# A 1024-to-4096-to-1024 MLP: fifteen instead of thirteen pairs by seven products, and fifteen tile remainders on GpSimd

## The chip, the cores and the metric

The kernel runs on one core of a Trainium2 chip, as one launch. The metric is the time of one execution on the device in microseconds; the number compared is the median over several executions. A core has a matrix engine (TensorE; PE in the profile, with its weight loads as PEld), three engines for elementwise work (VectorE, DVE; ScalarE, ACT; GpSimd, POOL) and SyncE (SP), which here issues the loads of weights. The engines run their own instruction lists and meet only at semaphores.

## The reference, cut to what matters

Two transformer blocks run one after the other on 256 tokens of width 1024, all in float32. The change is in the MLP that ends the first block:

```python
x = x + mix @ w_out[layer]
h = rmsnorm(x, norm_mlp[layer])
x = x + jnp.square(jax.nn.relu(h @ w_up[layer])) @ w_down[layer]   # 1024 -> 4096 -> 1024
```

The second block (norm `norm_mix_2`, projections `w_in_2`, ...) starts from this `x`.

## The kernel before

**Precision.** TensorE multiplies in a reduced format (fp32r). Each operand is therefore kept as two parts: a rounded one, `h`, and its remainder `l` = operand - `h`. One product takes three matmuls: h·h, h·l and l·h. For a tile of weights, ScalarE makes `h` (`round_tile`, line 1111) and VectorE makes `l` (`rest_of_tile`, line 1661).

**Tiles and rings.** `weight` asks for a tile of 512 KB. SyncE loads it into one of RAW = 4 slots of `raws`, in the order in which TensorE asks for tiles (line 2585); before it loads a slot again it waits until the tile that was there has its remainder (semaphore `lo`). `h` and `l` go to one of PARTS = 5 buffers of `parts`; ScalarE rounds tile i only when TensorE has released tile i-5. ScalarE and VectorE take all tiles in this one order. Between two pieces of other work, `until(v)` lets them first take the tiles whose buffer TensorE gives back before its event v; a tile whose buffer comes free exactly at v comes after that piece.

**The MLP.** The 4096 hidden columns are 16 pairs q of 256. For each pair TensorE computes `up(q)` from two tiles of `w_up` (48 matmuls of 256 columns). ScalarE takes relu and square of it (lines 1392, 1394) and rounds it (1399), VectorE makes the remainder (1695). Then pair q meets rows 256q to 256q+255 of `w_down`, in two tiles: `down(q, 0)` for output columns 0 to 511, `down(q, 1)` for 512 to 1023. TensorE runs up(q), down(q-2, 0), down(q-2, 1) in turn. The loop ends with up(15) and down(13, 0); then come down(14, 0), down(15, 0), down(13, 1), the transposes of the first half of the new x (`turn_x`, line 490), down(14, 1), down(15, 1).

**Seven products.** In the form with 12 matmuls of 512 columns (lines 806 to 808), down(q, 0) is a product of 2 x 2 blocks with eight block products. For the pairs in `by_sums` (1 to 13 here) `down_by_sums` takes seven, from sums of blocks: 21 matmuls of 256 columns (line 764). The sums of weight blocks are made by VectorE (`sums_of`, lines 1714 to 1718) and count as one more tile in the ring of five, rounded by ScalarE and given its remainder by VectorE. The sums of activation blocks are made by GpSimd (lines 2450 to 2454), rounded by ScalarE (1379) and given their remainder by VectorE. Two products are held in banks of their own; after the last pair by sums ScalarE copies one block (`first_copied`, 1384), VectorE adds the rest up (`join`) and adds all of the first half to x (line 1701). Only then may TensorE transpose it.

Of the kernel before, what the change touches and what calls it, by code (L numbers as in the profile page):

```python
# [48 lines left out]
    "qk_hi", "qk", "w_sums", "u_sums", "us_hi", "usT", "first_product", "joined",  # L49
# [10 lines left out]
class Tile:  # L60


    def __init__(self, i, srcs, k, n, raw, h, l):
        self.i, self.srcs, self.k, self.n = i, srcs, k, n
        self.raw, self.h, self.l = raw, h, l
        self.slot = self.load = self.before = None
        self.sums = self.nth_sums = None
        self.release = None
# [34 lines left out]
def build(nc, a, out):  # L103
    with ExitStack() as ctx:  # L104
# [123 lines left out]
        by_sums = [range(1, 14), range(1, 10)]  # L228
# [3 lines left out]
        us = [[chunks(v[:, :, :].rearrange("p c n -> p (c n)"), 4) for v in pair(17664 + 1024 * i, 2)] for i in range(4)]  # L232
        joint = f32(21760, 256)
# [74 lines left out]
        tiles, loaded, made = [], [], []  # L308
# [6 lines left out]
        def tensor(e):  # L315
# [39 lines left out]
            def weight(src, k, n, paired=False):  # L355

                i, slot = len(tiles), len(loaded) % RAW
                raw = raws[:, slot, 0:k * n].rearrange("p (k n) -> p k n", k=k)
                h, l = (parts[:, i % PARTS, j, 0:k * n].rearrange("p (k n) -> p k n", k=k) for j in range(2))
                if paired:  # L360
                    srcs = [(raw[64 * g:64 * g + 64], src[64 * k * g:64 * k * (g + 1), :].rearrange("(k p) n -> p k n", p=64))
                            for g in range(2)]
                else:
                    srcs = [(raw, src.rearrange("(k p) n -> p k n", p=P))]
                t = Tile(i, srcs, k, n, raw, h, l)
                t.slot, t.before = slot, loaded[-RAW] if len(loaded) >= RAW else None
                t.load = 16 * len(srcs) + (t.before.load if t.before else 0)
                tiles.append(t)
                loaded.append(t)
                return t  # L370
# [383 lines left out]
            def mlp(u, n, up, w_down):  # L754
# [12 lines left out]
                def down_by_sums(q):  # L767
# [15 lines left out]
                    product(c11, u12, w21)  # L783
# [10 lines left out]
                    sums.release = done(product(c21, u22, t4))  # L794

                def down(q, h):
# [3 lines left out]
                    w_ = weight(w_down[256 * q:256 * q + 256, 512 * h:512 * h + 512], 2, 512)  # L800
                    need(s["lo"], w_.i + 1)
                    for t in range(2):
                        ps, tok = psum[:, own[2 * h + t], :], slice(t * P, t * P + P)
                        for k in range(2):
                            wh, wl, (uh, ul) = w_.h[:, k, :], w_.l[:, k, :], ups[q % 4]
                            e.matmul(ps, uh[:, k, tok], wh, start=q == 0 and k == 0, stop=False)  # L806
# [7 lines left out]

                for q in range(2, n):
# [275 lines left out]
        def scalar(e):  # L1091
# [294 lines left out]

            def up(q):
                until(where["up", q].at)
                sums_rounded(0, q - 1)
# [9 lines left out]
                e.activation(ups[q % 4][0], r, ACT.Copy).then_inc(s["up_hi"], 1)  # L1399

            for q in range(16):
                up(q)
            first_copied(0)
# [240 lines left out]
        def vector(e):  # L1644
# [118 lines left out]

            def residual(name, u, factor=None, factor_in=None, n=0):
# [16 lines left out]
                if late:  # L1781
                    rest_of_tile()
                gains(u, 0, late)
                if late:
                    rest_of_tile()
                rests(u, 0)
                if late:
                    rest_of_tile()
# [4 lines left out]
                if late:  # L1793
                    rest_of_tile()
# [264 lines left out]
            for q in range(16):  # L2059
                r, name = tmps[q % 4], ("up", q)  # L2060
                until(where[name].at)
                sums_rest(0, q - 1)
                full(name)
                e.wait_ge(s["up"], q + 1)
                rest(r, ups[q % 4], "up_hi", q + 1, "upT")
            e.wait_ge(s["gain2"], 1)
# [346 lines left out]
        def gpsimd(e):  # L2413
# [41 lines left out]

            def all_up_sums(u):

                for q in by_sums[u]:
                    if u:
# [39 lines left out]
            all_up_sums(0)  # L2499
            e.wait_ge(s["xT"], 4 * MIX2 + 4)  # L2500
# [72 lines left out]
        def sync(e):  # L2573
# [100 lines left out]
```

## Time and profile before

| | us |
|---|---|
| median of 3 executions | 954.05 (953.63 to 955.58) |
| the profiled execution, its own time | 953.48 |
| its span in the trace | 951.3 |
| TensorE busy | 943.1 (99% of the span) |
| VectorE busy | 701.3 (74%) |
| ScalarE busy | 558.4 (59%) |
| GpSimd busy | 128.5 (14%) |

The span is what the trace covers; the 2.2 us by which the execution is longer lie around it. The MLP of the first block takes the stretch from 219 to 389 us. A time of the trace is counted from the start of the span.

### The profile page before, as it was taken

The page shows a single profiled execution, that of the slowest core. Times are in us where ns is not written, and L with a number is a line of the kernel's source. Part 1 is how long each engine was busy: PE and PEld are TensorE (multiplying, and loading weights), DVE is VectorE, ACT ScalarE, POOL GpSimd, SP SyncE. Part 2 cuts the span into 40 slices and gives each one's busy share as a digit, 9 for nine tenths or more (in the row PEclk, how much of TensorE's full clock was granted, in tenths as well). Part 3 has the DMA queues.
Part 4 walks back from the last instruction along what each step waited for, and adds up shares of the span by engine and source line. Part 5 has one row for each costly group of instructions (what it writes and reads, how often), then busy time and mean ns, then how long its engine had stood idle before and what let it go on. Part 6 is the DMA issues. An engine that isn't in the chain of part 4 may idle for free. (4 is left out here: it accounts for less than half of the span.)

```text
span 951.3 us, 16977 instructions
## 1 busy us (share of the span) xinstructions
PE 943.1 (99%) x6888; PEld 868.2 (91%) x6888; DVE 701.3 (74%) x934; ACT 558.4 (59%) x852; POOL 128.5 (14%) x178
## 2 busy tenths in 40 slices
PE   9999999999999999999999999999999999999997
PEld 7877999989999999989987999998998899999996
DVE  6767875777777887888866787776666467777777
ACT  6577554556666666656865674545455445555544
POOL 3000001004223320414000001100000012121210
PEclk9999999999999999999999999999999999999999
DMA  9974447555666666656565365555645346565661
GB/s 309 305 242 130 118 128 179 159 177 185 191 190 194 194 195 202 181 160 199 146 188 162 106 202 175 176 182 172 196 162 171 118 156 201 176 201 177 199 200 66
DMA packets 133549, 170.43 MB, mean 179 GB/s; under 512 B 5824, under 2 KB 97296, under 8 KB 133472
## 3 DMA queue, kind: packets, MB, share of 16 engines
q1 hardware_dynamic: 131408, 165.07, 55.9%
q10 hardware_dynamic: 1424, 2.84, 0.9%
q0 software_dynamic: 640, 1.44, 0.7%
q8 instruction: 54, 0.88, 0.4%
q14 instruction: 23, 0.19, 0.1%
HBM read 168.28 MB, written 1.05 MB: 178 GB/s over the span
## 5 line engine op out<-in xcount | busy, mean ns | idle before, releaser
L1661 DVE TENSOR_TENSOR parts<-raws,parts 128x1024 fp32r<-128x1024 f32 (+3 forms) x307 | 364.5, 1202 | 131.3 <-ACT parts L1111 130.4
L1111 ACT ACTIVATE parts<-raws 128x1024 fp32r<-128x1024 f32 (+3 forms) x307 | 309.3, 1029 | 129.2 <-PE ps L405 54.2
L403 PE MATMUL ps<-room_r,parts 128*128 128x256 f32 x1248 | 351.6, 282 | 0.0
L404 PE MATMUL ps<-room_r,parts 128*128 128x256 f32 x1248 | 348.6, 279 | 0.0
L405 PE MATMUL ps<-room_r,parts 128*128 128x256 f32 x1248 | 348.3, 279 | 0.0
L403 PEld LDWEIGHTS ps<-room_r,parts 128*128 128x128 f32 x1248 | 234.6, 188 | 2.2 <-issue 0.8
L404 PEld LDWEIGHTS ps<-room_r,parts 128*128 128x128 f32 x1248 | 234.7, 188 | 1.1
L405 PEld LDWEIGHTS ps<-room_r,parts 128*128 128x128 f32 x1248 | 234.7, 188 | 0.0
L434 PE MATMUL ps<-parts,room_r 128*128 128x512 f32 (+1 forms) x336 | 133.9, 399 | 0.8 <-DVE parts L1661 0.8
L435 PE MATMUL ps<-parts,room_r 128*128 128x512 f32 (+1 forms) x336 | 131.1, 390 | 0.0
L436 PE MATMUL ps<-parts,room_r 128*128 128x512 f32 (+1 forms) x336 | 131.1, 390 | 0.0
L434 PEld LDWEIGHTS ps<-parts,room_r 128*128 128x128 f32 x336 | 63.1, 188 | 16.2 <-DVE parts L1661 2.1
L436 PEld LDWEIGHTS ps<-parts,room_r 128*128 128x128 f32 x336 | 63.1, 188 | 14.4
L435 PEld LDWEIGHTS ps<-parts,room_r 128*128 128x128 f32 x336 | 63.2, 188 | 13.4 <-issue 0.5
L1695 DVE TENSOR_TENSOR room_r<-room,room_r 128x512 fp32r<-128x512 f32 (+1 forms) x71 | 49.4, 696 | 32.0 <-ACT room_r L1399 10.2
L764 PE MATMUL ps<-parts,room_r 128*128 128x256 f32 x462 | 58.1, 281 | 0.0
L764 PEld LDWEIGHTS ps<-parts,room_r 128*128 128x128 f32 x462 | 56.0, 188 | 0.0
L1111 ACT ACTIVATE parts<-room 128x1024 fp32r<-128x1024 f32 x22 | 23.4, 1062 | 55.2 <-DVE room L1718 30.1
L806 PE MATMUL ps<-parts,room_r 128*128 128x512 f32 x116 | 46.1, 397 | 0.0
L807 PE MATMUL ps<-parts,room_r 128*128 128x512 f32 x116 | 45.9, 395 | 0.0
L808 PE MATMUL ps<-parts,room_r 128*128 128x512 f32 x116 | 45.7, 394 | 0.0
L2450 POOL TENSOR_TENSOR room<-room 128x256 f32<-128x256 f32 x22 | 16.2, 738 | 207.9 <-DVE room L1695 116.3
(241 smaller groups left out, 1115.1 us busy)
## 6 DMA issues: line engine op xcount, KB each, us to landing
raws<-in_w_in SPq DMA_DIRECT2D x99, 512.0 KB, 4.4
raws<-in_w_ffn_in SPq DMA_DIRECT2D x44, 512.0 KB, 4.4
raws<-in_w_up SPq DMA_DIRECT2D x32, 512.0 KB, 3.9
raws<-in_w_down SPq DMA_DIRECT2D x32, 512.0 KB, 3.8
raws<-in_w_ffn_out SPq DMA_DIRECT2D x22, 512.0 KB, 4.4
raws<-in_w_xkv SPq DMA_DIRECT2D x16, 512.0 KB, 4.4
raws<-in_w_out SPq DMA_DIRECT2D x8, 512.0 KB, 4.3
raws<-in_w_up_ssd SPq DMA_DIRECT2D x8, 512.0 KB, 5.5
```

Of the source, the lines that this page charges most:

```text
L403: e.matmul(ps, wh, hT[0][:, k, :], start=k == 0, stop=False)
L404: e.matmul(ps, wh, hT[1][:, k, :], start=False, stop=False)
L405: last = e.matmul(ps, wl, hT[0][:, k, :], start=False, stop=k == K - 1)
L434: e.matmul(ps, hT[0][:, k, tok], wh, start=k == 0, stop=False)
L435: e.matmul(ps, hT[0][:, k, tok], wl, start=False, stop=False)
L436: last = e.matmul(ps, hT[1][:, k, tok], wh, start=False, stop=k == K - 1)
L764: last = e.matmul(ps, left[lh], right[rh], start=begins, stop=ends_)
L806: e.matmul(ps, uh[:, k, tok], wh, start=q == 0 and k == 0, stop=False)
L807: e.matmul(ps, uh[:, k, tok], wl, start=False, stop=False)
L1111: e.activation(t.h, t.raw, ACT.Copy).then_inc(s["hi"], 1)
L1661: e.tensor_tensor(t.l, t.raw, t.h.bitcast(F32), ALU.subtract).then_inc(s["lo"], 1)
L1695: return e.tensor_tensor(o, i0, i1, op)
```

## The change

1. For the first block's MLP `by_sums` covers pairs 0 to 14 instead of 1 to 13. Pair 15 stays in the usual form, with its first matmul into one bank split in two halves.
2. The second-half tiles of pairs 1 to 15 no longer go through the ring of five. `weight_apart` gives them a raw slot like any tile, but `h` and `l` lie in three places of their own. ScalarE rounds them in `apart_rounded`, one in each `up(q)` from q = 2 on, ahead of its work on up(q), and the last one after up(15). GpSimd makes their remainders in `rest_apart` (semaphore `own_lo`), each ahead of the activation sums of a pair, and the last two after all sums. SyncE waits for `own_lo` where the slot held such a tile.
3. TensorE asks for the tile of pair q-2 ahead of up(q) (from q = 3 on), for that of pair 14 ahead of down(14, 0) and for that of pair 15 ahead of down(15, 0). Loads are issued in that order.
4. VectorE's four remainders between the pieces of the residual (`rest_of_tile`) are now made only if the tile's buffer comes free in time (`due_rest`).

```diff
-        by_sums = [range(1, 14), range(1, 10)]
+        by_sums = [range(15), range(1, 10)]
+        at_apart = (10240, 12288, 24576)
...
+            def weight_apart(src):
+                slot, at = len(loaded) % RAW, at_apart[len(apart) % 3]
...
+                t.slot, t.before = slot, loaded[-RAW]
+                t.load = 16 + t.before.load
+                apart.append(t)
+                loaded.append(t)
...
-                    w_ = weight(w_down[256 * q:256 * q + 256, 512 * h:512 * h + 512], 2, 512)
-                    need(s["lo"], w_.i + 1)
+                    if h and q in asked:
+                        w_ = asked[q]
+                        need(s["own_lo"], w_.nth_apart)
+                    else:
+                        w_ = weight(w_down[256 * q:256 * q + 256, 512 * h:512 * h + 512], 2, 512)
+                        need(s["lo"], w_.i + 1)
...
                 for q in range(2, n):
+                    if q > 2:
+                        ask(q - 2)
                     up(q)
                     down(q - 2, 0)
                     if q < n - 1:
                         down(q - 2, 1)
+                ask(n - 2)
                 down(n - 2, 0)
+                ask(n - 1)
                 down(n - 1, 0)
...
+            def apart_rounded(n):
+                t = apart[n]
+                e.wait_ge(landed[t.slot], t.load)
+                if n >= 3:
+                    e.wait_ge(s["pe"], apart[n - 3].release)
+                e.activation(t.h, t.raw, ACT.Copy).then_inc(s["own_hi"], 1)
+
             def up(q):
                 until(where["up", q].at)
-                sums_rounded(0, q - 1)
+                if q > 2:
+                    sums_rounded(0, q - 1)
+                if q > 1:
+                    apart_rounded(q - 2)
                 full(("up", q))
...
             for q in range(16):
                 up(q)
+            apart_rounded(14)
             first_copied(0)
...
+            def due_rest(u):
+                if gives_back(lo) < where["tail", u].at:
+                    rest_of_tile()
...
+            def rest_apart(n):
+                t = apart[n]
+                e.wait_ge(s["own_hi"], n + 1)
+                e.tensor_tensor(t.l, t.raw, t.h.bitcast(F32), ALU.subtract).then_inc(s["own_lo"], 1)
...
                 for q in by_sums[u]:
+                    if u == 0 and q > 1:
+                        rest_apart(q - 2)
...
             all_up_sums(0)
+            for n in (13, 14):
+                rest_apart(n)
...
-                    e.wait_ge(s["lo"], t.before.i + 1)
+                    if t.before.nth_apart:
+                        e.wait_ge(s["own_lo"], t.before.nth_apart)
+                    else:
+                        e.wait_ge(s["lo"], t.before.i + 1)
```

Below, a tile D14 is the first-half tile of pair 14, S14 the sums made from it, H14 the second-half tile of pair 14 as the kernel before has it, A14 the same tile in the kernel after, and C0, C1, C2 are the first tiles of `w_in_2` for the next block.

ScalarE (ACT) at the end of the MLP. Before: D13 (its sums S13 in the row after), D14, D15, the three steps on up(15), H13, H14, the copy of the block for `join`:

```order
L1111 ACTIVATE parts<-raws 128x768 [waits s_pe,s_landed3]
L1111 ACTIVATE parts<-room 128x1024 [waits s_pe,s_w_sums]
L1111 ACTIVATE parts<-raws 128x1024 [waits s_pe,s_landed0]
L1111 ACTIVATE parts<-raws 128x1024 [waits s_pe,s_landed1]
L1392 ACTIVATE room<-ps 128x512 [waits s_pe]
L1394 ACTIVATE room<-room 128x512 [waits s_taken5]
L1399 ACTIVATE room_r<-room 128x512 [waits s_up,s_pe]
L1111 ACTIVATE parts<-raws 128x1024 [waits s_pe,s_landed2]
L1111 ACTIVATE parts<-raws 128x1024 [waits s_pe,s_landed3]
L1384 ACTIVATE room<-ps 128x256 [waits s_pe]
```

After: D14, S14, the sums of pair 14, the tile apart of pair 14 (A14), the three steps on up(15), A15, D15, C0, C1, C2, the copy:

```order
L1143 ACTIVATE parts<-raws 128x768 [waits s_pe,s_landed2]
L1143 ACTIVATE parts<-room 128x1024 [waits s_pe,s_w_sums]
L1411 ACTIVATE room_r<-room 128x512 [waits s_u_sums]
L1425 ACTIVATE room_r<-raws 128x1024 [waits s_pe,s_landed1]
L1435 ACTIVATE room<-ps 128x512 [waits s_pe]
L1437 ACTIVATE room<-room 128x512 [waits s_taken4]
L1442 ACTIVATE room_r<-room 128x512 [waits s_up,s_pe]
L1425 ACTIVATE room_r<-raws 128x1024 [waits s_pe,s_landed3]
L1143 ACTIVATE parts<-raws 128x1024 [waits s_pe,s_landed0]
L1143 ACTIVATE parts<-raws 128x1024 [waits s_pe,s_landed1]
L1143 ACTIVATE parts<-raws 128x1024 [waits s_pe,s_landed2]
L1143 ACTIVATE parts<-raws 128x1024 [waits s_pe,s_landed3]
```

D15 stood ahead of the steps on up(15) and now stands behind them and behind A15; three tiles of the next block now stand ahead of the copy that `join` waits for.

VectorE (DVE) at the same place, from the remainder of up(15) on. Before, D15 is already done there, and H13 and H14 come ahead of `join`:

```order
L1695 TENSOR_TENSOR room_r<-room,room_r 128x512 [waits s_up_hi,s_up,s_pe]
L1661 TENSOR_TENSOR parts<-raws,parts 128x1024 [waits s_hi,s_mlp_rstd,s_gain2]
L1661 TENSOR_TENSOR parts<-raws,parts 128x1024 [waits s_hi]
L1695 TENSOR_TENSOR room<-ps,room 128x256 [waits s_first_product]
L1695 TENSOR_TENSOR room<-room,ps 128x256 [waits s_dve_step]
```

After, D15 and then C0, C1 and C2 come ahead of `join`:

```order
L1741 TENSOR_TENSOR room_r<-room,room_r 128x512 [waits s_up_hi,s_up,s_pe]
L1707 TENSOR_TENSOR parts<-raws,parts 128x1024 [waits s_hi,s_mlp_rstd,s_gain2]
L1707 TENSOR_TENSOR parts<-raws,parts 128x1024 [waits s_hi] x3
L1741 TENSOR_TENSOR room<-ps,room 128x256 [waits s_first_product]
L1741 TENSOR_TENSOR room<-room,ps 128x256 [waits s_dve_step]
```

Two remainders behind up(15) have become four, and three of them are of tiles of the next block.

SyncE (SP) in the kernel after, from the load of A14 on: A14, D14 and A15, D15, then C0, C1, C2, C3:

```order
L2651 DMA raws<-in_w_down 128x2x512 [waits s_own_lo]
L2651 DMA raws<-in_w_down 128x2x512 [waits s_lo] x2
L2651 DMA raws<-in_w_down 128x2x512 [waits s_w_sums,s_lo]
L2651 DMA raws<-in_w_in_2 128x4x256 [waits s_own_lo]
L2651 DMA raws<-in_w_in_2 128x4x256 [waits s_w_sums,s_lo]
L2651 DMA raws<-in_w_in_2 128x4x256 [waits s_own_lo]
L2651 DMA raws<-in_w_in_2 128x4x256 [waits s_lo]
```

In the kernel before, the same place reads:

```order
L2585 DMA raws<-in_w_down 128x2x512 [waits s_w_sums,s_lo]
L2585 DMA raws<-in_w_down 128x2x512 [waits s_lo] x3
L2585 DMA raws<-in_w_down 128x2x512 [waits s_w_sums,s_lo]
L2585 DMA raws<-in_w_down 128x2x512 [waits s_lo]
L2585 DMA raws<-in_w_in_2 128x4x256 [waits s_lo] x4
```

The load of A14 waits for GpSimd's remainder of A13, that of C0 for A14's and that of C2 for A15's; each holds up the loads behind it.

## Rows read from the trace of the kernel before

**Rows 1.** The page: busy time of TensorE, and its granted clock in 40 slices.
```profile
PE 943.1 (99%) x6888; PEld 868.2 (91%) x6888; DVE 701.3 (74%) x934; ACT 558.4 (59%) x852; POOL 128.5 (14%) x178
PEclk9999999999999999999999999999999999999999
```
**Rows 2.** Waits of TensorE in the whole span: total us, times, longest.
```profile
PE ps L386 <- DVE junk L1842: 1.0, 1, 1.0
PE ps L434 <- DVE parts L1661: 0.8, 1, 0.8
```
**Rows 3.** Timeline of TensorE, both forms of down: start, us, what, count.
```profile
229.39 0.39 PE L806 MATMUL ps<-parts,room_r 128*128 128x512 f32 x1
...
240.58 2.65 PE L764 MATMUL ps<-parts,room_r 128*128 128x256 f32 x21
243.06 0.40 PE L806 MATMUL ps<-parts,room_r 128*128 128x512 f32 x1
...
245.86 0.28 PE L403 MATMUL ps<-room_r,parts 128*128 128x256 f32 x1
```
**Rows 4.** Busy time of the engines over one pair in the steady stretch.
```profile
251.45:262.33 10.88, 10.88 (x83) 10.34 (x82) 8.70 (x11) 7.02 (x10) 3.04 (x3) 1.00 0.64 193
```
**Rows 5.** Timeline of ScalarE at the start: the rounding of up(1).
```profile
226.53 0.63 ACT L1399 ACTIVATE room_r<-room 128x512 fp32r<-128x512 f32 x1
```
**Rows 6.** Timeline of ScalarE, last pairs: start, us, line, idle before.
```profile
360.17 0.61 ACT L1379 ACTIVATE room_r<-room 128x512 fp32r<-128x512 f32 x1
...
370.08 1.06 ACT L1111 ACTIVATE parts<-raws 128x1024 fp32r<-128x1024 f32 x1 [1.66 <-PE ps L405]
371.42 0.60 ACT L1392 ACTIVATE room<-ps 128x512 f32<-128x512 f32 x1 [0.27 <-PE ps L405]
...
372.78 0.63 ACT L1399 ACTIVATE room_r<-room 128x512 fp32r<-128x512 f32 x1
...
375.21 0.37 ACT L1384 ACTIVATE room<-ps 128x256 f32<-128x256 f32 x1
```
**Rows 7.** Timeline of TensorE at the end of the MLP.
```profile
371.22 2.65 PE L764 MATMUL ps<-parts,room_r 128*128 128x256 f32 x21
...
382.11 1.04 PE L490 MATMUL ps<-ident,x 128*128 128x128 f32 x8
```
**Rows 8.** Timeline of VectorE: sums of weight blocks, then join and adds.
```profile
364.78 0.69 DVE L1714 TENSOR_TENSOR room<-raws 128x512 f32<-128x512 f32 x1
...
366.30 0.95 DVE L1661 TENSOR_TENSOR parts<-raws,parts 128x768 fp32r<-128x768 f32 x1
...
376.77 0.42 DVE L1695 TENSOR_TENSOR room<-ps,room 128x256 f32<-128x256 f32 x1
...
379.67 1.41 DVE L1701 SCALAR_TENSOR_TENSOR x<-ps,ssq,x 128x512 f32<-128x512 f32 x2
```
**Rows 9.** Groups by form, 237 to 369 us: VectorE's remainder of a tile.
```profile
L1661 DVE TENSOR_TENSOR parts<-raws,parts 128x1024 fp32r<-128x1024 f32 x37 | 45.4, 1228 | 15.3 <-ACT parts L1111 15.3
```
**Rows 10.** Groups of GpSimd by form: its two-input operations, large and smallest.
```profile
L2450 POOL TENSOR_TENSOR room<-room 128x256 f32<-128x256 f32 x22 | 16.2, 738 | 207.9 <-DVE room L1695 116.3 <-ACT room L1394 91.6
...
L2515 POOL TENSOR_TENSOR ssq<-ssq 128x1 f32<-128x1 f32 x2 | 0.4, 186 | 0.0
```
**Rows 11.** SyncE's loads, 355 to 400 us: from issue to landing.
```profile
DMA to landing us min/median/max: 3.5/4.1/5.2
```
**Rows 12.** Timeline of ScalarE: two tiles rounded as they land.
```profile
401.82 1.06 ACT L1111 ACTIVATE parts<-raws 128x1024 fp32r<-128x1024 f32 x1 [2.75 <-DMA raws<-in_w_in]
403.20 1.06 ACT L1111 ACTIVATE parts<-raws 128x1024 fp32r<-128x1024 f32 x1 [0.32 <-DMA raws<-in_w_in]
```
**Rows 13.** Line 1714 on VectorE, all 22: ns, shortest, median, longest.
```profile
L1714 DVE TENSOR_TENSOR room<-raws x22: 677/944/951, 232.9 to 925.3; 128x512 f32<-128x512 f32 x22
```
**Rows 14.** End of the span: busy times, granted clock, DMA share, GB/s.
```profile
944.00:946.00 2.00, 1.05 (x9) 0.84 (x8) 1.26 (x3) 1.03 (x3) 0.78 (x3) 1.00 0.00 0
...
948.00:951.30 3.30, 0.00 (x0) 0.00 (x0) 0.16 (x1) 0.20 (x1) 0.00 (x0) 0.50 0.41 159
```

More of the change, by code:

```diff
@@ L66, in __init__ @@
         self.slot = self.load = self.before = None
-        self.sums = self.nth_sums = None
+        self.sums = self.nth_sums = self.nth_apart = None
         self.release = None
@@ L307, in build @@
         where = {}
-        tiles, loaded, made = [], [], []
+        tiles, loaded, made, apart = [], [], [], []
         def gives_back(i):
@@ L369, in weight @@
                 loaded.append(t)
+                return t
+            def weight_apart(src):
+                slot, at = len(loaded) % RAW, at_apart[len(apart) % 3]
+                raw = chunks(raws[:, slot, :], 2)
+                h, l = (chunks(room_r[:, i:i + 1024], 2) for i in (at, at + 1024))
+                t = Tile(None, [(raw, src.rearrange("(k p) n -> p k n", p=P))], 2, 512, raw, h, l)
+                t.slot, t.before = slot, loaded[-RAW]
+                t.load = 16 + t.before.load
+                apart.append(t)
+                loaded.append(t)
+                t.nth_apart = len(apart)
                 return t
@@ L782, in down_by_sums @@
                     product(p1, u11, w11, first)
-                    product(c11, u12, w21)
+                    product(c11, u12, w21, first and q == 0)
                     need(s["usT"], nth_sums[u][q] + 1)
@@ L793, in down_by_sums @@
                         ends(last, ("product", u, 1), sums_in[1])
-                    sums.release = done(product(c21, u22, t4))
+                    sums.release = done(product(c21, u22, t4, first and q == 0))
                 def down(q, h):
@@ L805, in down @@
                             wh, wl, (uh, ul) = w_.h[:, k, :], w_.l[:, k, :], ups[q % 4]
-                            e.matmul(ps, uh[:, k, tok], wh, start=q == 0 and k == 0, stop=False)
+                            if h == 0 and t and k == 0 and q == by_sums[u][-1] + 1 and 0 in by_sums[u]:
+                                for c in (slice(0, 256), slice(256, 512)):
+                                    e.matmul(ps[:, c], uh[:, k, tok], wh[:, c], start=False, stop=False)
+                            else:
+                                e.matmul(ps, uh[:, k, tok], wh, start=q == 0 and k == 0, stop=False)
                             e.matmul(ps, uh[:, k, tok], wl, start=False, stop=False)
@@ L813, in down, with ask @@
                         where["down", u, q] = Group(None, count, None)
+                asked = {}
+                def ask(q):
+                    if u == 0:
+                        asked[q] = weight_apart(w_down[256 * q:256 * q + 256, 512:D])
                 for q in range(2, n):
+                    if q > 2:
+                        ask(q - 2)
                     up(q)
```

18 lines of the change are left out of this document (12 added, 6 removed).

## The prediction

> **What bounds the kernel now.** First the page: TensorE is busy 99% of the span and its granted clock is full in every slice [rows 1]. Then its waits: in the whole span there are two, of 1.0 and 0.8 us [rows 2]. So nothing that another engine does faster can shorten this kernel; a gain has to come from fewer matmul columns, and any new wait of TensorE is a loss in full. Then the cost of the two forms of down: seven products take from 240.58 to 243.06, 2.48 us, the usual form from there to 245.86, 2.80 us [rows 3]. A pair in the steady stretch takes 10.88 us, in which VectorE is busy 8.70, ScalarE 7.02, GpSimd 3.04 [rows 4]. What is left to read is how far ahead of TensorE the others are at the end of the MLP, since there the order changes most. I count from T, the start of down(13, 0), which is 371.22 [rows 7]. Before, ScalarE rounds D15 at 370.08 (T-1.1), takes up(15) from 371.42 and ends with it at 373.41 (T+2.2) [rows 6]; TensorE needs D15 after one product by sums and one in the usual form, at T + 2.48 + 2.80 = T+5.3 [rows 3]. VectorE's join and adds run from 376.77 to 379.67 + 1.41 = 381.08, 4.3 us, and TensorE transposes x at 382.11 (T+10.9) [rows 7, 8]. The transposes thus have a cover of only 1.0 us.
>
> **What the change saves.** Two pairs go from 2.80 to 2.48 us: 2 x 0.32 = 0.64 us on TensorE, all of it on the path. The split matmul of pair 15 costs nothing: two of 256 columns for one of 512, and the two forms take 0.118 us for the one (2.48 / 21) and 0.233 for the other (2.80 / 12) [rows 3]. VectorE loses 15 remainders of 1.23 us [rows 9]; as TensorE does not wait for it, this is worth nothing by itself.
>
> **GpSimd's new step.** No row shows GpSimd on 128 x 1024. Its nearest row is 128 x 256 with two inputs, 0.74 us; its smallest two-input operation takes 0.19 [rows 10]. Below, it could be as fast as VectorE, 1.23 us [rows 9]; above, four times 0.74 = 2.95. I take the row with one fixed part: 0.19 + 4 x (0.74 - 0.19) = 2.4 us, which lies near the upper end because GpSimd's own row is the nearer one. The Trainium skill ("GPSIMD Engine Reference", section "Performance versus the Vector engine") gives 4497 ns for a float32 tensor_tensor of 2048, an estimate of 2.25 us for 1024; the sum below would be 0.3 us less by it. No run so far shows that size.
>
> **Steady stretch: no cost.** GpSimd has 3.04 + 2.4 = 5.4 us of work in 10.9. VectorE has 8.70 - 1.23 = 7.5 plus what GpSimd takes from it. That it takes something shows in line 1714: 677 ns at the shortest, 944 at the median, when GpSimd works beside it [rows 13]. Even if VectorE stands for the whole new step it has 7.5 + 2.4 = 9.9 of 10.9 us. The ring of five now serves four tiles a pair, so it runs further ahead. ScalarE's work on up(q) starts 1.6 us later (sums 0.6, tile apart 1.0), but up(q) is needed only two pairs on. I take 0.
>
> **Start: no cost, at most 0.5.** Pair 0 now needs its sums at 229.39 + 0.7 us. ScalarE's work on up(1) ends at 227.16 [rows 5], and the rounding (0.6) and remainder (0.7) of the sums fit behind it; GpSimd's 3.0 us for them [rows 4] run from the square of up(0), a whole step of ScalarE earlier. Tighter is the second tile of up(3), which ScalarE rounds after up(2), its sums and the first tile apart: by the lengths of such steps it is ready within 0.5 us of when TensorE wants it (229.39 + 2.48 + 2.80 + 1.40 = 236.07) [rows 3]. I take 0 and keep 0.5 for the range.
>
> **End of the MLP: here the change loses.** Three things meet, all in the order of the lists. (a) The load of A14 waits for GpSimd's remainder of A13, and D14's load stands behind it. A13 is rounded around up(14), whose matmuls end at T-10.9. ScalarE rounds up(15)'s second tile, the sums and A13 until T-9.4; GpSimd is done at T-7.0; A14 is issued then, D14 some 1.1 later, and lands after 4.1 us and behind A14 [rows 11], the landings being 1.4 us apart (401.82, 403.20) [rows 12]: T-1.5. (b) VectorE makes the sums of D14, 1.6 us (364.78 to 366.30, with a little idle) [rows 8]: T+0.1. ScalarE rounds S14 (1.06), the sums of pair 14 (0.6), A14 (1.0), and only then takes up(15), 2.0 us [rows 6]: T+4.7. A15 follows, T+5.7, then D15, T+6.7; VectorE needs 1.23 [rows 9]: D15 is ready at T+7.9, or up to T+9.3 if GpSimd's remainder of A15 holds VectorE. TensorE wants it at T + 2 x 2.48 = T+5.0. **First new wait: 3 to 4 us.** (c) join now stands behind C0, C1 and C2 on VectorE, and the block's copy behind them on ScalarE. C2's load waits for the remainder of A15: rounded T+5.7, GpSimd 2.4 and a little to start, T+8.2; issued, landed after 4.1: T+12.4; rounded and the block copied (0.37) [rows 6]: T+13.8; VectorE's remainder of C2 T+14.7; join and adds 4.3 [rows 8]: **T+19.0**. TensorE would be there at T+7.9 + 5.6 = T+13.5 to T+14.9 and waits again, **4 to 5 us**, for x. Transposes at T+19.0 instead of T+10.9 is 8.1 us late. The saving on pair 14 is swallowed by these waits; that on pair 0 stays, 0.32. Behind the transposes the work is that of before, and the tiles of the next block are further ahead. The sum is 8.1 - 0.3 = +7.8 us, on the profiled execution's 953.48: 961.3. The median of the runs is 0.57 above that execution: **961.8 us**, 0.8% slower.
>
> **Bounds of it.** Low: D14 lands in time and S14 is rounded when its buffer comes free, as D15's was at T-1.1 [rows 6], which takes 1.25 off; GpSimd at 1.23 takes 1.2 off, a landing of 3.5 [rows 11] 0.6: +4.7, 958.8. High: GpSimd at 2.95 twice, +1.1; landings of 5.2 twice, +2.2; 0.5 at the start: +11.6, 965.6.
>
> **Rivals.** (1) **The change works as it says and costs nothing**: -0.64 us, 953.4, no change that can be told. It needs D15 ready by T+5.0 and join begun by T+10.5 - 4.3 = T+6.2. Even with loads and GpSimd at no cost, ScalarE reaches D15 at T+4.4, since up(15) and A15 stand ahead of it, so it is ready at T+6.6; that speaks against it. It is right if I misread which tiles stand where. Chance 0.07. The same reading error with a lower end than that is all that is left for a real gain, 0.03. (2) **The clock falls in the waits.** At the end of the span TensorE stops at 945.05, the granted clock is still 1.00 up to 946 and is 0.50 (1.2 GHz) from 948 [rows 14]: an idle of some 3 us was followed by the lower level. The second wait here is 4 to 5 us. If the 5.6 us of matmuls behind it run at the lower level in part, it costs up to 5.6 us, say half: 961.8 + 2.8 = 964.6. Against it: if the clock falls in the first wait already, down(15, 0) and down(13, 1) fill part of the second and the price vanishes in it. Chance 0.20. (3) **VectorE becomes the bound of the steady stretch**, held by GpSimd: it decides from a GpSimd step over 10.9 - 7.5 = 3.4 us, outside my bounds; at 4 us it costs 0.6 us in 13 pairs, 8 us on top, 970. The Trainium skill ("SBUF — State Buffer", section "SBUF: two separate sides") says that the shared port pair is an exclusive lock for the whole instruction, against a VectorE operation with two SBUF inputs; by it VectorE does stand for the full step, which I have counted, and the first wait is the longer one of the two I give, with the same end at T+19.0. The lengthened rows of line 1714 agree. Chance 0.05.
>
> **How the numbers follow.** The forecast (the sum with its bounds) 0.65, clock 0.20, VectorE 0.05, nothing 0.07, a gain 0.03. A measurement of this kernel can tell 0.2%, 1.9 us, from no change. Faster 0.03, same 0.07, slower 0.90. The range takes in the bounds of the sum and the clock rival: 958.3 to 966.5; outside it are the other three and the tail of the sum.
>
> **What would show it.** In the profile after, TensorE has two new waits between 373 and 391 us: for a tile's remainder by VectorE (line 1707) ahead of the last usual down, and for VectorE's adds (line 1747) ahead of the transposes; before 370 us it has none above 0.5 us. Seven products are 315 + 189 = 504 matmuls instead of 462 in all. GpSimd's row of 128 x 1024 reads 1.2 to 3.0 us, 15 times. The transposes start some 19 us after down(13, 0). The prediction is wrong if TensorE still has no wait there, if the waits lie in the steady stretch, or if the second wait ends on something other than the load of a `w_in_2` tile.

## The result, and the profile after the change

The changed kernel takes **987.83 us** (median, 986.55 to 989.27) against 953.85 for the kernel before, a ratio of 1.035 (95% interval 1.034 to 1.037): 34 us slower, where 961.8 with a range of 958.3 to 966.5 was predicted. The direction was right and the size was not. The profiled execution took 986.55 us, its span is 984.6.

The page of the changed kernel, TensorE's busy time and its granted clock in 40 slices (against [rows 1]), and the group of GpSimd's new step:

```profile
PE 955.4 (97%) x6907; PEld 876.5 (89%) x6907; DVE 707.8 (72%) x929; ACT 562.8 (57%) x856; POOL 163.2 (17%) x199
PEclk9999999999999999899999999999999999999999
...
L2513 POOL TENSOR_TENSOR room_r<-raws,room_r 128x1024 fp32r<-128x1024 f32 x15 | 39.1, 2606 | 102.4 <-ACT room_r L1425 102.4
```

TensorE is idle for 29.2 us of the span (984.6 - 955.4), 8.2 before. Its busy time grew too, by 12.3 us, though it has less to compute; one slice shows a lower clock, and more on this stands below. GpSimd's step takes 2.61 us on average. The waits of TensorE (against [rows 2]; total us, times, longest):

```profile
PE ps L778 <- DVE parts L1707: 14.1, 11, 2.1
PE ps L828 <- DVE parts L1707: 2.7, 1, 2.7
PE ps L504 <- DVE x L1747: 1.5, 1, 1.5
```

The last two are the two foreseen waits. The first was not foreseen: eleven waits before seven products (line 778). Nine of them, nearly one a pair, lie between 263 and 369 us, two at 394.16 and 398.23. The timeline of TensorE in the steady stretch and at the end (against [rows 7]; start, us, what, idle before):

```profile
263.06 3.08 PE L778 MATMUL ps<-parts,room_r 128*128 128x256 f32 x21 [0.35 <-DVE parts L1707]
...
394.16 3.07 PE L778 MATMUL ps<-parts,room_r 128*128 128x256 f32 x21 [1.56 <-DVE parts L1707]
398.23 0.95 PE L778 MATMUL ps<-parts,room_r 128*128 128x256 f32 x6 [1.00 <-DVE parts L1707]
...
406.41 0.47 PE L828 MATMUL ps<-parts,room_r 128*128 128x512 f32 x1 [2.66 <-DVE parts L1707]
...
415.26 1.31 PE L504 MATMUL ps<-ident,x 128*128 128x128 f32 x8 [1.55 <-DVE x L1747]
```

down(13, 0) starts at 394.16, it was 371.22: **22.9 us are lost in the steady stretch**. The transposes start 21.1 us behind it, they were 10.9: **10.2 us are lost at the end of the MLP**. Together 33.1, of a span that grew by 33.3.

**Why every pair is late.** The timelines of ScalarE, GpSimd and SyncE over one pair, from one tile apart (line 1425) to the next:

```profile
255.43 1.05 ACT L1425 ACTIVATE room_r<-raws 128x1024 fp32r<-128x1024 f32 x1
...
265.14 1.06 ACT L1143 ACTIVATE parts<-raws 128x1024 fp32r<-128x1024 f32 x1 [2.00 <-DMA raws<-in_w_up]
266.63 1.06 ACT L1143 ACTIVATE parts<-raws 128x1024 fp32r<-128x1024 f32 x1 [0.43 <-DMA raws<-in_w_up]
267.59 0.62 ACT L1411 ACTIVATE room_r<-room 128x512 fp32r<-128x512 f32 x1
268.11 1.05 ACT L1425 ACTIVATE room_r<-raws 128x1024 fp32r<-128x1024 f32 x1
```
```profile
256.56 2.58 POOL L2513 TENSOR_TENSOR room_r<-raws,room_r 128x1024 fp32r<-128x1024 f32 x1 [8.15 <-ACT room_r L1425]
```
```profile
259.17 0.37 SPq L2651 DMA_DIRECT2D raws<-in_w_down  x1
259.58 1.03 SPq L2651 DMA_DIRECT2D raws<-in_w_up  x2
```

Read in order of time this is a closed round: a chain of steps whose last one releases its first. ScalarE rounds a tile apart (to 256.48). GpSimd makes its remainder (to 259.14). Now the raw slot is free, and SyncE issues the next tile apart (259.17) and, only behind it in its list, the two tiles of `w_up` (259.58). They land some 5.6 us later; ScalarE stands idle for them, 2.00 and 0.43 us, rounds both (265.14, 266.63) and the sums, and behind them comes the next tile apart (268.11). The round takes 12.68 us, and TensorE's pair 10.88 [rows 4]. Nothing in it is busy all the time; each step waits for the one before. From 242.09 to 398.74 line 1425 takes 12 such steps, 13.05 us each on average. 12 x (13.05 - 10.88) = 26 us, and 22.9 reach TensorE; that the lead of the loads covers the other 3 is my reading, since its first wait of this kind is at 263.06.

**The clock.** The windows of TensorE (us, busy and count of PE, PEld, DVE, ACT, POOL, then granted clock, DMA share, GB/s):

```profile
313.00:315.00 2.00, 0.16 (x1) 0.19 (x2) 1.71 (x4) 1.06 (x1) 0.52 (x1) 0.99 1.07 257
315.00:317.00 2.00, 2.00 (x11) 2.00 (x11) 1.17 (x1) 0.00 (x0) 0.00 (x0) 0.50 0.94 331
...
401.00:403.00 2.00, 2.00 (x11) 2.00 (x11) 1.19 (x1) 1.99 (x3) 1.74 (x2) 0.50 0.00 0
```

At 314.84 TensorE comes out of a wait of 2.08 us, and its granted clock is 0.50 (1.2 GHz) in the next window. There are five such spells in the MLP, of some 3.4 us each, which cost about half their length: 8 to 9 us of the 12.3 by which the busy time grew. Most of the rest is a wait that the profile counts as busy. In the pairs that wait at full clock the seven products take 3.08 us and not 2.65 [rows 3]: in the pair of 263.06 TensorE stands for 0.4 us behind the ninth matmul, until VectorE has the remainder of the weight sums at 264.40. Seven such pairs make 3 us.

### The profile page after: what moved, and what is told of

Same layout as the page of the kernel before. It is cut to its first block, busy times and chain, and to the rows that moved or that the text cites. A ratio compares the mean times of both kernels' runs of the same rounds, so it can differ in the third digit from the quotient of the medians.

```text
span 984.6 us, 17040 instructions
## 1 busy us (share of the span) xinstructions
PE 955.4 (97%) x6907; PEld 876.5 (89%) x6907; DVE 707.8 (72%) x929; ACT 562.8 (57%) x856; POOL 163.2 (17%) x199
## 4 chain that ended last, share of the span: by engine, by line
PE 78%; issue 10%; POOL 7%; DVE 2%; DMA 2%; ACT 1%; SPq 0%; POOLq 0%; ACTq 0%; DVEq 0%
PE ps L417 12%; PE ps L419 12%; PE ps L418 12%; PE ps L448 8%; PE ps L449 8%; PE ps L450 8%; PE ps L400 4%; POOL room_r L2513 3%; PE ps L504 3%; PE ps L778 3%; POOL room L2503 1%; PE ps L828 1%; PE ps L829 1%; PE ps L830 1%; POOL room L2505 1%
## 5 line engine op out<-in xcount | busy, mean ns | idle before, releaser
L1707 DVE TENSOR_TENSOR parts<-raws,parts 128x1024 fp32r<-128x1024 f32 (+3 forms) x292 | 347.1, 1204 | 145.1 <-ACT parts L1143 144.3
L1143 ACT ACTIVATE parts<-raws 128x1024 fp32r<-128x1024 f32 (+3 forms) x292 | 294.8, 1028 | 145.7 <-DMA raws<-in_w_up 36.1
L1741 DVE TENSOR_TENSOR room_r<-room,room_r 128x512 fp32r<-128x512 f32 (+1 forms) x73 | 59.5, 818 | 43.6 <-ACT room_r L1442 23.0
L778 PE MATMUL ps<-parts,room_r 128*128 128x256 f32 x504 | 72.7, 301 | 16.1 <-DVE parts L1707 14.1
L778 PEld LDWEIGHTS ps<-parts,room_r 128*128 128x128 f32 x504 | 67.2, 204 | 20.2 <-issue 16.2
L448 PEld LDWEIGHTS ps<-parts,room_r 128*128 128x128 f32 x336 | 63.1, 188 | 16.5 <-DVE parts L1707 2.4
L450 PEld LDWEIGHTS ps<-parts,room_r 128*128 128x128 f32 x336 | 63.1, 188 | 14.4
L449 PEld LDWEIGHTS ps<-parts,room_r 128*128 128x128 f32 x336 | 63.2, 188 | 13.4 <-issue 0.5
L1143 ACT ACTIVATE parts<-room 128x1024 fp32r<-128x1024 f32 x24 | 25.4, 1059 | 65.5 <-DVE room L1764 39.1
L2513 POOL TENSOR_TENSOR room_r<-raws,room_r 128x1024 fp32r<-128x1024 f32 x15 | 39.1, 2606 | 102.4 <-ACT room_r L1425 102.4
L2487 POOL TENSOR_SCALAR ssq<-ssq 128x1 f32<-128x1 f32 x10 | 6.4, 637 | 253.5 <-ACT junk L1188 253.2
L2527 POOL TENSOR_SCALAR ssq<-ssq 128x1 f32<-128x1 f32 (+2 forms) x10 | 2.9, 291 | 252.6 <-ACT junk L1384 121.9
L2503 POOL TENSOR_TENSOR room<-room 128x256 f32<-128x256 f32 x24 | 23.9, 995 | 117.4 <-DVE room L1741 116.3
```

The costliest lines, as they stand in the source:

```text
L448: e.matmul(ps, hT[0][:, k, tok], wh, start=k == 0, stop=False)
L449: e.matmul(ps, hT[0][:, k, tok], wl, start=False, stop=False)
L450: last = e.matmul(ps, hT[1][:, k, tok], wh, start=False, stop=k == K - 1)
L778: last = e.matmul(ps, left[lh], right[rh], start=begins, stop=ends_)
L1143: e.activation(t.h, t.raw, ACT.Copy).then_inc(s["hi"], 1)
L1707: e.tensor_tensor(t.l, t.raw, t.h.bitcast(F32), ALU.subtract).then_inc(s["lo"], 1)
```

## The experiments

Two theories were set up on the steady stretch. R: the closed round above. P: VectorE is held while GpSimd works, and that is what makes TensorE late. Then come the runs on the end of the MLP.

**Tiles apart alone.** `by_sums` as before:

```diff
-        by_sums = [range(15), range(1, 10)]
+        by_sums = [range(1, 14), range(1, 10)]
...
-            for n in (13, 14):
+            for n in (12, 13, 14):
                 rest_apart(n)
```

> The change without its two added pairs: seven products for pairs 1 to 13 as before, fifteen tiles apart by GpSimd. Theory R: the round stays, 12.7 us a pair, 984 to 990 in all. Rival P: the same. Rival S: about 954.

Measured: 987.16 us (ratio 1.035, 1.032 to 1.037). The whole loss is that of the tiles apart.

**Fifteen pairs by sums alone.** No tiles apart; all remainders by VectorE (the calls of `apart_rounded` and `rest_apart` go too):

```diff
-                    if u == 0:
-                        asked[q] = weight_apart(w_down[256 * q:256 * q + 256, 512:D])
+                    pass
...
-                if q > 1:
-                    apart_rounded(q - 2)
...
-                    if u == 0 and q > 1:
-                        rest_apart(q - 2)
```

> The change without its tiles apart: fifteen pairs by seven products, every second-half tile back in the ring of five with its remainder by VectorE. Theory R (a closed round: ScalarE rounds a tile apart, GpSimd makes its remainder 2.6 us, only then SyncE issues the next tile apart and behind it the two up tiles, they land 5 to 6 us later, ScalarE rounds them and only then the next tile apart; 12.7 us a pair against TensorE's 10.9): no such round here, so no wait of TensorE before 370 us and a time of 953 to 955. Rival P (GpSimd's long operation holds VectorE through the shared port, and VectorE is late): the same, since GpSimd has no long operation. Rival S (the seven products of pair 0 or 14 bring the waits): 980 or more.

Measured: 956.96 us (1.0033, 1.0022 to 1.0045). TensorE has no wait before 370 us, but the kernel is 3 us slower, which I return to below.

**The load behind up.** The only edit of the changed kernel is the place in SyncE's list:

```diff
-                    if q > 2:
-                        ask(q - 2)
                     up(q)
+                    if q > 2:
+                        ask(q - 2)
```

> The whole change, but each tile apart is asked for behind up(q) and not ahead of it, so SyncE issues the two up tiles before it waits for GpSimd's remainder. GpSimd and VectorE do all that they do in the change. Theory R: the round is open, a pair takes 10.9 us again and only the waits at the end of the MLP stay, 8 to 10 us: 961 to 965. Rival P: 12.7 us a pair stay, 985 to 990.

Measured: **960.62 us** (1.007, 1.005 to 1.009). GpSimd's steps are all still there, and 27 us are gone. The timelines of SyncE and of ScalarE in this kernel:

```profile
252.42 1.50 SPq L2651 DMA_DIRECT2D raws<-in_w_up  x2
256.42 4.14 SPq L2651 DMA_DIRECT2D raws<-in_w_down  x2
```
```profile
252.32 1.05 ACT L1425 ACTIVATE room_r<-raws 128x1024 fp32r<-128x1024 f32 x1
...
263.07 1.05 ACT L1425 ACTIVATE room_r<-raws 128x1024 fp32r<-128x1024 f32 x1
```

The `w_up` loads go out before GpSimd's remainder is done, and the period is 10.75 us in this pair and 10.82 in the next ones: TensorE sets it again. VectorE is busy 8.5 us and GpSimd 5.0 us of each pair. R holds, P is refuted for a step of 2.6 us. What is left is the end of the MLP. The waits of TensorE in this kernel:

```profile
PE ps L828 <- DVE parts L1707: 4.1, 1, 4.1
PE ps L504 <- DVE x L1747: 0.7, 1, 0.7
```

**Half of the step, round closed.** GpSimd makes the remainder of one of the two blocks of rows; TensorE uses it for both, so that the output is not the reference's:

```diff
-                            wh, wl, (uh, ul) = w_.h[:, k, :], w_.l[:, k, :], ups[q % 4]
+                            wh, wl, (uh, ul) = w_.h[:, k, :], w_.l[:, 0 if h and q in asked else k, :], ups[q % 4]
...
-                e.tensor_tensor(t.l, t.raw, t.h.bitcast(F32), ALU.subtract).then_inc(s["own_lo"], 1)
+                e.tensor_tensor(t.l[:, 0], t.raw[:, 0], t.h[:, 0].bitcast(F32), ALU.subtract).then_inc(s["own_lo"], 1)
```

> The changed kernel, order of the loads as in it (round closed), but GpSimd makes the remainder of only half of each tile apart (columns of the first block of 128 rows), so its step is some 1.3 us instead of 2.6; TensorE multiplies by the first block's remainder in both places, so its work has the same shape and the output is not the reference's. Theory R (closed round: tile rounded, remainder, load issued, w_up loads behind it, rounded): the round is 13.05 - 1.3 = 11.75 us, still over 10.88, so (11.75 - 10.88) x 12 = 10 us come from the stretch and some 5 to 6 at the end: 967 to 972, starts of the tiles apart 11.6 to 11.9 us apart. Rival P (the loss is VectorE's, which stands for GpSimd): VectorE has 7.5 + 1.3 = 8.8 of 10.9, no loss in the stretch: 957 to 961. Rival Q (the number of loads and queues, not GpSimd's step, sets it): 985 to 988, as the changed kernel.

Measured: 972.30 us (969.48 and 975.12). GpSimd's step is 1.50 us, and line 1425 comes 11.65 us apart (241.40 to 381.21 in 12 steps). The period follows GpSimd's step, 1.4 us less for 1.1 us less of it, as in R. The two executions are 5.6 us apart, and the median lies just over the 967 to 972 of theory R; the period is the better measure.

**The remainder by VectorE, round closed.** `rest_apart` moves to VectorE's list, ahead of its wait for up(q), and out of GpSimd's:

```diff
+                if q > 1:
+                    rest_apart(q - 2)
                 full(name)
```

> The whole change with the same order of loads and roundings, but VectorE and not GpSimd makes the remainders of the tiles apart (1.2 us in place of 2.6), so nothing long runs on GpSimd. Theory R: the round is shorter by 1.4 us only, 11.3 us a pair, 5 us over the 12 pairs, and the waits at the end are 2 to 3 us shorter: 962 to 972. Rival P: a pair takes 10.9 us and the time is that of the waits at the end, 957 to 961.

Measured: 970.21 us (968.58 and 971.84), period 11.7 where 11.3 was expected. GpSimd does nothing new here, and the stretch still loses: the round is closed over VectorE instead. Of the 34 us, 18 hang on who makes the remainder and how long it takes.

**The step twice, load behind up.** GpSimd makes every remainder two times:

```diff
+                step(e.tensor_tensor(t.l, t.raw, t.h.bitcast(F32), ALU.subtract))
+                settle()
                 e.tensor_tensor(t.l, t.raw, t.h.bitcast(F32), ALU.subtract).then_inc(s["own_lo"], 1)
```

> The changed kernel with the load of the tile apart issued behind the two loads of w_up (as in the run that gave 960.62), and with GpSimd making each of the 15 remainders twice over, so that its step per pair is about 5.2 us instead of 2.6; the output is unchanged. The round through SyncE is open here, so its length should not matter. Theory L (VectorE stands while GpSimd runs a two-input step): VectorE has 7.5 + 5.2 = 12.7 us of a pair of 10.9, it becomes the bound, some 1.8 us in each of 12 pairs, +22, and +2.6 to 5 at the end: 980 to 988, with starts of the tiles apart on ScalarE 12.4 to 12.9 us apart. Theory F (VectorE stands for a part of GpSimd's step only, one or two operations of it): the stretch keeps 10.9 us and only the end grows by 2.6 to 5.2 us: 963 to 967.

Measured: 988.50 us, just over the range of theory L; line 1425 is 12.3 us apart, just under it. The timelines of VectorE and GpSimd in this kernel:

```profile
320.78 1.57 DVE L1741 TENSOR_TENSOR room_r<-room,room_r 128x512 fp32r<-128x512 f32 x1 [1.24 <-ACT room_r L1442]
322.28 2.89 DVE L1760 TENSOR_TENSOR room<-raws 128x512 f32<-128x512 f32 x1
```
```profile
318.86 2.95 POOL L2513 TENSOR_TENSOR room_r<-raws,room_r 128x1024 fp32r<-128x1024 f32 x1 [4.22 <-ACT room_r L1425]
321.88 2.73 POOL L2515 TENSOR_TENSOR room_r<-raws,room_r 128x1024 fp32r<-128x1024 f32 x1
```

An operation of VectorE that takes 0.68 us elsewhere in this stretch ends at 322.35, behind GpSimd's first step (321.81); its sum of weight blocks, 0.68 us when alone [rows 13], ends at 325.17, behind the second (324.61). So VectorE stands for the whole of GpSimd's instructions, one by one. It is not full though: it has 1.24 us of idle time a pair, waiting for ScalarE. By the timelines the round is closed again by another way: tile apart rounded, GpSimd's two steps, VectorE's sums held until they end, ScalarE's rounding of these sums and of two tiles, next tile apart (317.73 to 330.07). No run tests this second round by itself. L gave the right size for a reason that is half of it.

**The order at the end of the MLP, load behind up too.** ScalarE and VectorE take D15 in up(15), and ScalarE copies the block before it rounds the last two tiles apart (the same edit as the next one, beside the load behind up):

> The whole change with two orders altered: each tile apart is asked for behind up(q), as in the run that opened the round, and at the end of the MLP ScalarE and VectorE take D15 ahead of up(15), the block's copy and join ahead of C0, C1 and C2, and A14 and A15 behind the copy. GpSimd does all its work. If both losses are orders, nothing of them is left: no wait of TensorE in the MLP above 0.5 us, 953.2 to 954.5. If GpSimd's share of the port costs by itself, VectorE's join is late and waits of 1 us or more stay at the transposes: 956 or more.

Measured: 961.56 us (1.0081, 1.0066 to 1.0096), no better than 960.62. VectorE and GpSimd there:

```profile
377.52 5.18 DVE L1752 SCALAR_TENSOR_TENSOR x<-room,ssq,x 128x512 f32<-128x512 f32 x2
```
```profile
376.96 5.20 POOL L2521 TENSOR_TENSOR room_r<-raws,room_r 128x1024 fp32r<-128x1024 f32 x2 [10.37 <-ACT room_r L1427]
```

The join is at 376.06, 0.7 us earlier than in the kernel before. But then two adds that took 1.41 us [rows 8] take 5.18: GpSimd's remainders of the last two tiles run at the same time. The first transposes come at 383.55, 1.4 us later than before. The larger wait stands behind them:

```profile
PE ps L504 <- DVE x L1752: 5.6, 2, 3.9
```

1.7 us of it is the wait for the first half of x and 3.9 that for the second. In the second, ScalarE has five tiles of `w_in_2` ahead of the rounding of x, which it starts at 390.49. The loads of the first and the third of them go out only when GpSimd's two remainders end (379.36 and 382.16). Behind the second wait TensorE runs 6.8 us at 0.50 of its clock, from 392.88. So both the port and the loads cost here, and the loads more.

**The same order at the end, load as in the changed kernel:**

```diff
-                if q > 1:
+                if q == 15:
+                    round_tile()
+                elif q > 1:
                     apart_rounded(q - 2)
...
-            apart_rounded(14)
             first_copied(0)
+            apart_rounded(13)
+            apart_rounded(14)
...
+                if q == 15:
+                    rest_of_tile()
                 full(name)
```

> The change with its loads in its own order (the closed round stays) and only the order at the end of the MLP altered as above. If the two losses add up, the steady stretch keeps its 22 us and the waits at the end, about 10 us, go: 976 to 980. If the waits at the end are there only because everything is late, it stays at 984 to 988.

Measured: 987.57 us, no gain. The first transposes do come earlier, at 409.81 instead of 415.26, but the second ones at 420.57 instead of 421.89, after a wait of 3.9 us: the raw slots of the next tiles wait for GpSimd's last two steps. From 421.56 TensorE then runs 3.4 us at 0.50 of its clock, which takes back the last 1.3 us.

**The last two tiles back in the ring.** As the run with both orders, but the second-half tiles of pairs 14 and 15 are rounded and given their remainder as before (GpSimd's and ScalarE's last steps for them go too):

```diff
-                    if u == 0:
+                    if u == 0 and q < 14:
```

> As the run with both orders, but the second-half tiles of pairs 14 and 15 stay in the ring of five with their remainders by VectorE, so that C0 and C2 do not wait for GpSimd. If the loads behind A14 and A15 still cost in the run with both orders, this one is faster than it by that, 953.2 at best; if they do not, both are the same.

Measured: **957.26 us** (1.0038, 1.0023 to 1.0052), 4.3 us better than with both orders. The edit takes away both GpSimd's last steps beside the adds and the loads that waited for them, so it does not part the two. The first transposes start at 382.21, as before the change. Most of what is left begins on ScalarE:

```profile
385.95 1.06 ACT L1143 ACTIVATE parts<-raws 128x1024 fp32r<-128x1024 f32 x1 [5.72 <-DMA raws<-in_w_in]
386.92 1.13 ACT L1198 ACTIVATE room_r<-big 128x512 fp32r<-128x512 f32 x2
```

A tile that has not landed stands ahead of the rounding of x, and TensorE waits 1.9 us for the second half of x. Behind that wait its clock is 0.50 for 3.4 us, and it waits 1.0 us more at line 535.

**Fifteen pairs by sums, with that order at the end,** no tiles apart:

> No tiles apart; fifteen pairs by seven products, with D15 ahead of up(15) and the copy and join ahead of H14, H15 and C0. The run without tiles apart had its waits (0.7 to 1.5 us) at the transposes and at the next block's first tile. If these come from the order alone, they go, and the 0.64 us of the two pairs can be seen: 953.0 to 953.8. If the ring of five itself is too short with two more tiles of sums, a wait stays: 955 or more.

Measured: 975.35 us (1.0228), a miss by 22 us, and 18 worse than without the order. The waits of TensorE:

```profile
PE ps L828 <- DVE parts L1707: 9.6, 3, 4.7
PE ps L535 <- DVE parts L1707: 4.3, 1, 4.3
```

The timeline of VectorE shows why:

```profile
380.54 1.22 DVE L1707 TENSOR_TENSOR parts<-raws,parts 128x1024 fp32r<-128x1024 f32 x1
386.89 1.29 DVE L1741 TENSOR_TENSOR big<-ps,final_col 128x512 f32<-128x512 f32 x2 [5.14 <-PE ps L504]
388.10 1.22 DVE L1707 TENSOR_TENSOR parts<-raws,parts 128x1024 fp32r<-128x1024 f32 x1
394.62 1.29 DVE L1741 TENSOR_TENSOR room_r<-big,room_r 128x512 fp32r<-128x512 f32 x2 [5.31 <-ACT room_r L1197]
395.84 1.22 DVE L1707 TENSOR_TENSOR parts<-raws,parts 128x1024 fp32r<-128x1024 f32 x1
```

ScalarE has rounded the second-half tiles by 380, but join now stands ahead of their remainders, and VectorE makes these one by one between the pieces of the residual. Each piece waits for something that comes behind the remainder before it: the transposes, then the rounding of x behind a load whose raw slot the remainder frees (ScalarE is idle 5.65 and 6.34 us for two tiles of `w_in_2`). TensorE goes on at 381.81, 389.37 and 397.11, each time as one of these remainders ends.

**Pair 0 alone by sums,** `range(14)`, no tiles apart:

> Only one part of the change: by_sums[0] is range(14), so pair 0 is made by seven products and pair 14 is not; no tiles apart, all remainders by VectorE. Together with the kernel that has both pairs by sums and nothing else (956.96) this parts pair 0 from pair 14. Theory E (the end of the MLP is where fifteen pairs by sums cost, pair 0 costs nothing): the saving of one pair stays, 0.32 us, so 953.3 to 953.9, with no TensorE wait over 0.4 us around 230 to 240 us. Rival A (the start costs what was lost): 955.5 to 957, with a wait of TensorE in the first pairs. If A were right, the missing 3 us of that other kernel would lie at the start and not at the end.

Measured: 954.82 us (1.001, 1.0001 to 1.0019): neither the gain nor rival A. No wait in the first pairs. VectorE and ScalarE do the same as before up to 389 us; then one remainder is missing in VectorE's list (the fourth of those between the pieces of the residual), and TensorE waits 1.5 us for it at line 535. That is part 4 of the change, `due_rest`, which the prediction did not price.

**The same with all four remainders:**

```diff
-                    due_rest(u)
+                    rest_of_tile()
```

> The kernel with pair 0 alone by seven products (954.82) with one part of the change undone in it: VectorE makes all four remainders of the next block's tiles between its steps behind the MLP, as the kernel before does, instead of only those that the condition calls due. Theory D (that condition postpones the fourth remainder, at 389.4 us in the kernel before, and TensorE's wait of 1.5 us for it at the next block is what pair 0 alone cost): the wait goes, 953.3 to 953.9, no wait of TensorE for a remainder over 0.4 us behind the MLP. Rival N (that wait is an effect of the ring's order and stays): 954.6 to 955.1. Whether pair 0 itself saves its 0.32 us shows in the distance to the kernel before: 0.3 less, or nothing if TensorE waits that long for the sums of pair 0.

Measured: **953.20 us** against 953.68 in the same series, a ratio of 0.9996 (0.9987 to 1.0005). The two timelines of VectorE, first with `due_rest`, then with all four:

```profile
388.76 0.75 DVE L1743 SCALAR_TENSOR_TENSOR x<-ps,ssq,x 128x512 f32<-128x512 f32 x1 [0.60 <-PE ps L830]
389.43 0.68 DVE L1737 TENSOR_TENSOR big<-ps,final_col 128x512 f32<-128x512 f32 x1
```
```profile
388.81 0.75 DVE L1743 SCALAR_TENSOR_TENSOR x<-ps,ssq,x 128x512 f32<-128x512 f32 x1 [0.60 <-PE ps L830]
389.48 1.22 DVE L1703 TENSOR_TENSOR parts<-raws,parts 128x1024 fp32r<-128x1024 f32 x1
```

Postponing one step of 1.22 us cost 1.6 us. So of the 3 us of the fifteen pairs, `due_rest` is some 1.6 (it stands in that kernel too, with the same wait of 1.5 us at line 535), and pair 14 with D15 behind up(15) some 1.9 (3.04 over the kernel before in its series, less 1.16 in its own). Pair 0 was to be worth 0.32 us by its matmuls; 0.48 was measured, and the interval cannot tell it from nothing.

## Why the prediction was wrong

**"Steady stretch: no cost"** is the step that failed, with 22.9 of the 26 us by which the forecast missed. It compared sums: GpSimd 5.4 of 10.9 us, VectorE at most 9.9. Both sums were right (5.0 and 8.5 us a pair were measured where the load stands behind up) and say nothing on a round. The runs showed the closed round in its place, 13.05 us a pair. "The ring of five now serves four tiles a pair, so it runs further ahead" looked at the buffers for parts; the four raw slots behind it, loaded in one order, bound it. The same section priced the same chain at the end of the MLP ("the load of A14 waits for GpSimd's remainder of A13, and D14's load stands behind it"), and did not ask what it does in every pair. With the prediction's own terms it could have been had: tile apart rounded 1.0, GpSimd 2.4, the first of three loads landed after 4.1 and the other two 1.4 us apart [rows 11, 12], the last of them rounded 1.06, sums 0.6: 12.0 us, 1.1 over a pair and some 13 us in 12 of them. The rest of the 12.7 to 13 us is slower landings (a median of 6.2 us for `w_up`, 3.9 before) and GpSimd's 2.6.

**The saving** could not be told from nothing by itself: 0.48 us for pair 0, with an interval from a gain of 1.2 to a loss of 0.5.

**GpSimd's step** was put at 2.4 (1.23 to 2.95, from [rows 9, 10]) and takes 2.61. The Trainium skill ("GPSIMD Engine Reference", section "Performance versus the Vector engine") gave an estimate of 2.25; the trace is 16% above it.

**Start: no cost, at most 0.5.** Right, with a small cost where the prediction saw the tightest place: TensorE waits 0.34 us for the second tile of up(3) at 236.53 in the changed kernel. Where GpSimd makes its step twice that wait is 2.17 us.

**End of the MLP** was right in its mechanism and near in its size, best seen where the load stands behind up and the stretch costs nothing: the first wait is 4.1 us (3 to 4 predicted), transposes come 18.15 us after down(13, 0) at 370.92 (19.0 predicted), and the kernel takes 960.62 (961.8 predicted). The chain is the forecast one: ScalarE starts on C2 as it lands at T+12.2 (landing at T+12.4 predicted) and join starts at T+14.5 (T+14.7). The second wait is 0.7 and not 4 to 5. The clock is 0.50 from 378.72 to 385.55, so the matmuls between the waits take 8.2 us and not 5.6: this is rival 2 in the form in which its price vanishes in the second wait. TensorE goes on after the first wait at T+9.2, near the late end of its T+7.9 to T+9.3, and the transposes start after three of the four adds, not after all, 0.8 us sooner than the T+19.0. In the changed kernel itself, the transposes are at T+21.1 with waits of 2.7 and 1.5, and there are two more of 1.0 each in down(14, 0), which the sum did not have. D14 is later than its T-1.5:

```profile
395.61 0.85 ACT L1143 ACTIVATE parts<-raws 128x768 fp32r<-128x768 f32 x1 [1.37 <-DMA raws<-in_w_down]
```

That is T+1.4. Its load waits for GpSimd's remainder of A13, as predicted, but A13 is later against T than the sum had it, as ScalarE rounds it behind a `w_up` tile that lands late (GpSimd ends with it at T-3.9, not T-7.0). So the step that failed in the steady stretch seems to be behind the 2 us by which the T+19.0 is off as well; no run tests that alone.

**`due_rest`** was left out of the sum, without a reason. It cost 1.6 us where it was tested alone; in the changed kernel TensorE has no wait at line 535, and what it costs there was not measured.

**Rival 3** (VectorE held by GpSimd, from a step over 3.4 us, chance 0.05) named the place of the loss and the wrong cause. The lock itself is real. The Trainium skill ("SBUF — State Buffer", section "SBUF: two separate sides") calls the port pair an exclusive lock for the whole instruction; the traces agree, with 5.18 us for two adds of 1.41 beside 5.20 of GpSimd. But at 2.6 us it cost nothing in the steady stretch. At 5.7 us it cost 1.4 us a pair; by the timelines through a round, not by a full VectorE, which no run tested by itself.

## What to carry to other kernels

When a step moves to another engine, follow what its end releases once around until the same step comes again, and compare that length with the pair, besides the busy sums: an order of loads in one queue ties engines together that share no data. A slow producer that frees a load slot belongs behind the urgent loads in that queue; here one such line was worth 27 of 34 us. An order that looks better for one wait can delay the slots behind it, so look at the loads of the next stage before it is taken, and at what the other holder of a shared port does at that moment.

## What the runs showed of the hardware

Short waits can be enough for the lower clock, and their length alone does not decide it. In the changed kernel TensorE waited 1.24, 1.31 and 1.45 us in three pairs in a row at clock 1.00; the waits of 2.08, 1.90 and 2.03 us (before 314.84, 341.53 and 368.13) were each followed by some 3.4 us at 0.50, and so was a group of three, 1.56, 1.00 and 1.04, from 394 to 400. With half of GpSimd's step two waits of 0.80 and 1.04 us before 380.71 and 382.70 were followed by 3.4 us at 0.50. With GpSimd's step twice it waited 2.17 us before 238.55 and 1.2 us in each of 11 pairs, and the clock stayed at 1.00 up to 401 us.

An operation of VectorE with two inputs in SBUF that starts while GpSimd runs such an instruction ends behind it by nearly its own length: 0.54 and 0.56 us for two of 0.68 (with GpSimd's step twice), and 1.1 for one of 1.23 (403.67 + 2.59 = 406.26 in the changed kernel, GpSimd having ended at 405.18).

Loads of 512 KB of `w_up` land after a median of 3.9 us in the kernel before, where loads go out 2 to 3.4 us apart, after 6.2 us in the changed kernel, where three go out within 1.5 us, and after 4.7 us with the load behind up.
